# An RWKV pair loop written out flat, its state update folded into one operation, and a bias table made at the start of a hybrid layer

## The reference, cut to what matters

```python
def _wkv_step(S, inp):                                  # RWKV-7: 16 heads, state 64 x 64
    r, w, k, v, a, b = inp
    sa = jnp.einsum('bhvk,bhk->bhv', S, a)
    S = S * w[:, :, None, :] + sa[..., None] * b[:, :, None, :] + v[..., None] * k[:, :, None, :]
    return S, jnp.einsum('bhvk,bhk->bhv', S, r)

def one_block(args):                                    # sparse attention, a block of 128 queries
    ...
    score = jnp.einsum('bths,bth->bts', jax.nn.relu(dots), iws)
    _, idx = lax.top_k(score, topk)
    ...
    logits = jnp.einsum('btngd,btsnd->btngs', qg, ks) * (HD_B ** -0.5)
    bias = rel_bias[_t5_bucket(idx - ps[None, :, None])]
    logits = jnp.where(sel_ok, logits + bias, -jnp.inf)

mixed = (gates[:, :, 0] * (o_a @ lw['p_a']) + gates[:, :, 1] * (o_b @ lw['p_b'])
         + gates[:, :, 2] * (o_m @ lw['p_m']))
h = x + mixed @ lw['w_o']
h = h + _hier_moe(_rmsnorm(h, lw['g_ffn']), lw)
```

## Time and profile before

| | us |
|---|---|
| median of 3 runs | 2541.69 |
| lowest and highest run | 2533.03, 2544.68 |
| profiled execution, its time | 2558.45 |
| its span (first to last instruction) | 2556.9 |
| PE busy | 2334.8 (91%), 13394 matmul instructions |
| DVE, ACT, POOL busy | 532.3, 312.4, 43.2 |

### The profile page before, as it was taken

One profiled execution on the slowest core, in us unless ns is written; L12 is line 12 of the kernel. 1 busy time (PEld: TensorE's weight loads), 2 busy tenths in 40 slices (PEclk: granted clock), 3 DMA queues, 4 the chain that ended last, 5 costly groups with the idle time before them and its releaser, 6 DMA issues.

```text
span 2556.9 us, 32554 instructions
## 1 busy us (share of the span) xinstructions
PE 2334.8 (91%) x13394; PEld 1612.1 (63%) x13394; DVE 532.3 (21%) x1457; ACT 312.4 (12%) x696; POOL 43.2 (2%) x88
## 2 busy tenths in 40 slices
PE   6999999947998999999999999999798999899887
PEld 4887776725756776776777777777454554455444
DVE  1000001233553232232232232200400111011103
ACT  4010001112222011011010110000201100010002
POOL 0000000001000000000000000000000000000000
PEclk9999999968887999999999999999879978897998
DMA  7554443343221323133133232344159769576972
GB/s 236 179 165 132 133 122 121 99 70 113 79 66 39 100 72 104 46 124 104 35 103 102 70 101 99 130 132 173 49 205 364 280 254 373 227 308 273 365 307 88
DMA packets 222911, 392.57 MB, mean 154 GB/s; under 512 B 10784, under 2 KB 165200, under 8 KB 221664
## 3 DMA queue, kind: packets, MB, share of 16 engines
q1 hardware_dynamic: 217712, 382.16, 42.1%
q0 software_dynamic: 3984, 7.83, 1.6%
q10 hardware_dynamic: 1088, 0.66, 0.1%
HBM read 382.32 MB, written 8.29 MB: 153 GB/s over the span
## 4 chain that ended last, share of the span: by engine, by line
PE 82%; DMA 6%; DVE 3%; ACT 2%; issue 2%; another core or an unknown queue 2%; DVEq 1%; ACTq 0%; POOL 0%; SPq 0%
PE bank L822 15%; PE bank L662 10%; PE bank L1035 7%; PE bank L684 7%; DMA ring<-in_w 5%; PE bank L824 5%; PE bank L1054 5%; PE bank L965 5%; PE bank L1083 5%; PE bank L635 4%; PE bank L953 3%; PE bank L1104 2%; PE bank L878 1%; PE bank L886 1%
## 5 line engine op out<-in xcount | busy, mean ns | idle before, releaser
L822 PE MATMUL bank<-uT,ring 128*128 128x288 f32 x1536 | 420.2, 424 | 0.0
L822 PEld LDWEIGHTS bank<-uT,ring 128*128 128x128 f32 x1536 | 290.2, 195 | 84.7 <-issue 4.4
L662 PE MATMUL bank<-uT,ring 128*128 128x288 f32 (+2 forms) x1024 | 248.9, 406 | 0.7 <-ACTq L315 0.7
L662 PEld LDWEIGHTS bank<-uT,ring 128*128 128x128 f32 (+2 forms) x1024 | 190.5, 186 | 58.8 <-ACTq L315 0.9
L684 PE MATMUL bank<-uT,ring 128*128 128x288 f32 x768 | 215.5, 428 | 0.0
L1035 PE MATMUL bank<-SC,Z 128*128 128x128 f32 (+1 forms) x768 | 184.9, 385 | 8.9 <-ACT SC L1389 5.6
L1054 PE MATMUL bank<-ring,Z 128*64 128x512 f32 x768 | 172.1, 604 | 17.0 <-DMA ring<-in_w 15.7
L684 PEld LDWEIGHTS bank<-uT,ring 128*128 128x128 f32 x768 | 148.0, 200 | 44.4 <-issue 6.6
L1035 PEld LDWEIGHTS bank<-SC,Z 128*128 128x128 f32 (+1 forms) x768 | 141.7, 247 | 51.2 <-issue 34.9
L1054 PEld LDWEIGHTS bank<-ring,Z 128*64 128x64 f32 x768 | 64.1, 139 | 122.9 <-issue 122.6
L824 PE MATMUL bank<-Z,ring 128*128 128x288 f32 x512 | 138.9, 417 | 2.0 <-issue 2.0
(11 more groups left out here) (339 smaller groups left out, 2208.1 us busy)
## 6 DMA issues: line engine op xcount, KB each, us to landing
ring<-in_w SPq DMA_DIRECT2D x64, 2048.0 KB, 18.1
ring<-in_w_in SPq DMA_DIRECT2D x102, 1024.0 KB, 7.8
SC<-in_w SPq DMA_DIRECT2D x32, 2048.0 KB, 15.9
ring<-in_w_mem_kv SPq DMA_DIRECT2D x16, 1024.0 KB, 10.1
ring<-in_w_o SPq DMA_DIRECT2D x16, 1024.0 KB, 7.7
ring<-in_p_b SPq DMA_DIRECT2D x8, 1024.0 KB, 5.6
ring<-in_p_m SPq DMA_DIRECT2D x8, 1024.0 KB, 8.1
ring<-in_p_a SPq DMA_DIRECT2D x8, 1024.0 KB, 7.4
```

The lines of the kernel that those rows point to most:

```text
L662: ins = mm(bank[t][0:w, 0:T], rslot[q][:, c, w0:w0 + w], uT[:, c, :], start=c == 0, stop=c == KC - 1)
L822: ins = mm(b[:, 0:T], rslot[q][:, c, P * t:P * t + P], uT[:, c, :], start=c == 0, stop=c == last - 1)
```

## The change

**The pair loop.** All five engines' loops over the pairs are Python loops now, so the instructions of eight pairs stand one after the other, and wait targets are constants. The loops of the other stages stay.

**The state update.** A vector `sx` is made once in a pair (`ee[c] * em[c+1]` for the chunks 0 to 2, `ee[c]` for 3 and 4). After `rw_s0` DVE makes `S1 = S0 * sx[c]`. When the increment has come, one operation makes `bank4 * sx[c] + S1`.

**The order of heads.** Where two or three matmuls of one head stood together (L906 and L907, L919 and L920, L923 to L925), first both heads' first matmul is issued, then both heads' second.

**Two dense groups.** Five groups instead of four stand before `rw_hat`, and one stands after the last chunk's outputs, ahead of `rw_fin`. Three are left after the variance.

**The bias.** `onehot`, `relb` and `brow` lie in `NK` now, which stage 5 alone uses otherwise. They are loaded first of all, the two matmuls are PE's first work (banks 0 and 1), the copies DVE's first, and POOL writes `bias_rows` once `xT_done` is set, at the end of the first transposes. Only the eight loads of `E` wait for stage 3's end.

```diff
-        brow = cut(SC, 0, BW)
-        onehot = cut(SC, BW, BW)
-        relb = cut(SC, 2 * BW, 8)
         NK_t = sb("NK", PAIRS * T)
         vis = cut(NK_t, 0, 2 * TP)
+        brow = cut(NK_t, 2 * TP, BW)
+        onehot = cut(NK_t, 2 * TP + BW, BW)
+        relb = cut(NK_t, 2 * TP + 2 * BW, 8)
...
+            pload(onehot[0:32, :], a["onehot"], "past_in")
+            pload(relb[0:32, :], a["rel_bias"], "past_in")
             for k in (1, 2, 3, 4):
                 phase_end(pool, k)
+            pool.wait_ge(s("brow_done"), 1)
             pload(vis, a["visible"], "past_in")
-            phase_wait(pool, 3)
...
+            pool.wait_ge(s("xT_done"), 1)
             pload(dram_bias, brow[0:H_B, :].unsqueeze(1).to_broadcast([H_B, P, BW]), "brow_out")
             pool.wait_ge(s("brow_out"), 16)
-
+            phase_wait(pool, 3)
             for h in range(H_B):
...
+            pe.wait_ge(s("past_in"), 32)
+            mm(bank[0][0:H_B, 0:512], relb[0:32, :], onehot[0:32, 0:512], start=True, stop=True)
+            mm(bank[1][0:H_B, 0:BW - 512], relb[0:32, :], onehot[0:32, 512:BW], start=True, stop=True).then_inc(s("prep_mm"), 1)
...
-            pe.wait_ge(s("past_in"), 48)
             pe.wait_ge(s("past_hw"), 64)
...
-            mm(bank[7][0:H_B, 0:512], relb[0:32, :], onehot[0:32, 0:512], start=True, stop=True)
-            mm(bank[3][0:H_B, 0:BW - 512], relb[0:32, :], onehot[0:32, 512:BW], start=True, stop=True).then_inc(s("prep_mm"), 1)
-            pe.wait_ge(s("prep_done"), 2)
+            ins.then_inc(s("prep_mm"), 1)
+            pe.wait_ge(s("prep_done"), 1)
...
-            with pe.Fori(0, PAIRS) as j:
+            for j in range(PAIRS):
...
-                merge_mms(4)
+                merge_mms(5)
...
                     for hs in halfs:
                         mm(bank[2][hs, 0:CH], RA[hs, c, 0, :], S0[hs, :], start=True, stop=False)
+                    for hs in halfs:
                         ins = mm(bank[2][hs, 0:CH], Gm[hs, c, 1, 0:CH], tokm[hs, c, :], start=False, stop=True)
...
                 ins.then_inc(s("rw_y"), 1)
+                merge_mms(1)
...
+                V.tensor_tensor(vec["sx"][:, 0:3], vec["ee"][:, 0:3], vec["em"][:, 1:4], ALU.mult)
+                V.tensor_copy(vec["sx"][:, 3:5], vec["ee"][:, 3:5])
...
                     dve.sem_inc(s("rw_s0"), 1)
+                    V.tensor_scalar(S1, S0, vec["sx"][:, c:c + 1], None, ALU.mult)
...
-                    V.tensor_tensor(S1, S0, bank[4][:, 0:CH], ALU.add)
-                    dr()
-                    if c < 3:
-                        V.tensor_scalar(S0s[:, (c + 1) % 2, :], S1, vec["ee"][:, c:c + 1], vec["em"][:, c + 1:c + 2], ALU.mult, ALU.mult)
-                    else:
-                        V.tensor_scalar(SF[:, c - 3, :], S1, vec["ee"][:, c:c + 1], None, ALU.mult)
+                    after = S0s[:, (c + 1) % 2, :] if c < 3 else SF[:, c - 3, :]
+                    V.scalar_tensor_tensor(after, bank[4][:, 0:CH], vec["sx"][:, c:c + 1], S1, ALU.mult, ALU.add)
```

More of the change, by code:

```diff
@@ L151, in build @@
                         ("omka", 8), ("ss", 5), ("rs", 5), ("iw", 48),
-                        ("mx8", 8), ("nmax", 4), ("sum", 4), ("rsum", 4), ("last", 54), ("em", 5), ("ee", 5),
+                        ("mx8", 8), ("nmax", 4), ("sum", 4), ("rsum", 4), ("last", 54), ("em", 5), ("ee", 5), ("sx", 5),
                         ("eps", 2)):
@@ L428, in _ @@
                 strip(R_PAIR + q, merge_strips(0, q))
-            with sp.Fori(1, PAIRS) as j:
+            for j in range(1, PAIRS):
                 for q in range(4):
                     sp.wait_ge(s("mg_mm"), 10 * j + (MG_LAST[q] - 10))
-                    settle(sp)
                     for d_, s_ in merge_strips(j, q)(q):
@@ L521, in _, with pload @@
             pool.memset(vec["eps"][:, 0:1], LNX_EPS)
+            def pload(dst, src, name):
+                return pool.dma_start(dst, src).then_inc(s(name), 16)
+            pload(onehot[0:32, :], a["onehot"], "past_in")
+            pload(relb[0:32, :], a["rel_bias"], "past_in")
             for k in (1, 2, 3, 4):
                 phase_end(pool, k)
-            def pload(dst, src, name):
-                return pool.dma_start(dst, src).then_inc(s(name), 16)
+            pool.wait_ge(s("brow_done"), 1)
             pload(vis, a["visible"], "past_in")
-            phase_wait(pool, 3)
-            pload(onehot[0:32, :], a["onehot"], "past_in")
-            pload(relb[0:32, :], a["rel_bias"], "past_in")
-            pool.wait_ge(s("brow_done"), 1)
+            pool.wait_ge(s("xT_done"), 1)
             pload(dram_bias, brow[0:H_B, :].unsqueeze(1).to_broadcast([H_B, P, BW]), "brow_out")
             pool.wait_ge(s("brow_out"), 16)
+            phase_wait(pool, 3)
             for h in range(H_B):
@@ L565, in pair_in @@
                 cs = bass.ds(j * P, P)
-                if not isinstance(j, int):
+                if j:
                     pool.wait_ge(s("rw_lora"), j)
@@ L583, in _ @@
             pair_in(0)
-            with pool.Fori(0, PAIRS - 1) as j:
+            for j in range(PAIRS - 1):
                 pair_in(j + 1)
@@ L1310, in _ @@
             A(kn, kn, ACT.Sqrt).then_inc(s("kn_rt"), 1)
-            with act.Fori(0, PAIRS) as j:
+            for j in range(PAIRS):
                 def gate(u):
@@ L1431, in _ @@
             V.memset(vec["ss"], 1.0).then_inc(s("ss_init"), 1)
+            dve.wait_ge(s("prep_mm"), 1)
+            V.tensor_copy(brow[0:H_B, 0:512], bank[0][0:H_B, :])
+            V.tensor_copy(brow[0:H_B, 512:BW], bank[1][0:H_B, 0:BW - 512])
+            dr()
+            dve.sem_inc(s("brow_done"), 1)
             for k, part in enumerate((slice(0, 3), slice(3, 5))):
@@ L1599, in bc @@
                 return ap.unsqueeze(1).to_broadcast([P, n, ap.shape[-1]])
-            with dve.Fori(0, PAIRS) as j:
+            for j in range(PAIRS):
                 def pv(name):
```

10 lines of the change are left out of this document (2 added, 8 removed).

## The result

The changed kernel takes 2455.66 us in the median of 4 runs (2453.21 to 2471.07), the kernel before 2543.18 beside it (4 runs, 2533.03 to 2564.01): a ratio of 0.9658, 95% interval 0.9586 to 0.9731, some 87 us faster. The forecast was 2468, with 2448 to 2490 as its range. The time lies inside and the sign is right, but the sum behind it holds errors that cancel, and by the traces some 10 of the 87 us lie behind the last stage that the change touches.

What follows compares the result with a forecast made beforehand. PE is full nearly everywhere, so only its idle or low-clock time can be won: 39.7 + 2.3 - 1.6 + 18.3 + 9.9 + 4.3 + 1.0 = 73.9 us off the 2541.7 median gives 2468 us, range 2448 to 2490.

Steps and rivals of the forecast that it cites:

- wait for E, bias matmuls: Around stage 4: writing `bias_rows` 400 us earlier removes DVE's 39.7 us wait and 2.3 us of bias matmuls.
- state update: Pair loop: one operation behind the increment saves 0.31 us in 32 chunks, 9.9 us; bounds 6.4 and 12.1.
- groups, with the one ahead of `rw_hat`: Pair loop: group ahead of `rw_fin` covers 5.4 us, net 4.3 after mode changes; group ahead of `rw_hat` covers 1.0.
- The other rivals: Stalls stay, 2486 us (0.15); new wait at pair's head, 2476 (0.10); bias late, 2508 (0.03); slower, up to 2580 (0.03).
- The wait ahead of L906's successor 0.1 us or less.: Pair loop: sign that PE's wait for DVE's new state, 12.1 us over 32 times before, nearly goes.
- That cover holds.: Stage 1: beside the 53.8 us write, at 22.5 us a strip, the ring falls back 1.5 of three strips; no loss.
- a strip that PE waits for in the first 130 us: Stage 1: listed among the signs that would prove the prediction wrong.
- strips starve: Stage 1 rival: write and strips slow each other to twice their times; 32 us lost, 2500 us; chance 0.07.
- 1.6 us lost: Stage 4: E loads beside the index-key loads delay the keys by 4.8 - 3.2 = 1.6 us; bounds 0 and 5.2.
- 18.3 us: Pair loop: gain from removing jumps and the lower clock behind them, 16.95 in six pairs plus 1.3; bounds zero and 18.3.
- the pair taken as clean: Pair loop: the last pair, 99.20 us at clock 1.0, less the longest stall, 1.6, gives 97.6 without a jump.
- So I take zero: Pair loop: alternating heads at L906 and L907 gains between zero and 4.8 us; zero taken, 0.26 seeming mostly mode change.

Runs made afterwards that it cites:

- both repairs: Changed kernel with the bias write made from 128 partitions at its early place and E loads held until the index keys land: 2445.34 us, ratio 0.9679.
- the second profile: The kernel before, unchanged, profiled once more: pair loop 807.8 us, stage 4 to the first pair 283.0, experts 669.0 against 705.8 in its first profile.

## Why the prediction was right, and where it was wrong

| term | forecast, us | measured, us | by |
|---|---|---|---|
| wait for E, bias matmuls | 42.0 | 38.6 to 43.4 | both repairs: 244.4 from stage 4 to the first pair, against 283.0 and 287.8 before |
| keys beside E | -1.6 | -2.9 (-2.3 to -4.9 over all profiles) | L727; the keys put first |
| write beside stage 1 | 0 | -5.9 | L636; the write moved, and made wide |
| jumps | 18.3 | 25.0 (27.1 against the second profile) | loops written out only |
| state update | 9.9 | 10.3 | undone alone |
| groups, with the one ahead of `rw_hat` | 5.3 | 5.5 | undone alone |
| order of heads | 0 | 2.2 | undone alone |

**Right.** What bounds the kernel was read right: the wait at L1556 and the jump were the two large ones, and both went whole. The state update and the groups came within 0.4 us, each with some luck. For the update I had taken the merged operation at L1717's 0.22 us; it took 0.28, and the drain, which I had not counted, went too. In the groups' 5.3 us stands 1.0 for the wait ahead of `rw_hat`, which is gone with the jumps already: PE's waits list none there with the loops written out alone, nor with the groups back. The other rivals fell: no new wait stands at the pair's head, E is not late, and the "issue" that the waits list within the written-out pairs, 0.2 us at L905 once in each, stood at L906 before.

**"The wait ahead of L906's successor 0.1 us or less."** This sign did not come: 32 waits make 6.6 us, 0.2 each. With the old order of heads only 1.6 us are left, so the sign failed because alternation brings PE there sooner, which I had not put into it.

**"That cover holds."** This step failed, and with it the zero of the moved write. It took 22.5 us for a strip beside the write from the earlier trace rows, a median of two loads. One of them took 35.0 us, as the DMA view of 550 to 578 us before shows, so the other took 2 x 22.5 - 35.0 = 10.0:

```profile
ring<-in_w_in SPq DMA_DIRECT2D x1, 1024.0 KB, 35.0
```

SP's timeline has the issues of both:

```profile
547.79 5.23 SPq L420 DMA_DIRECT2D ring<-in_w_in  x2
```

The long one landed at 547.79 + 35.0 = 582.8 or later, when the write (done before 577.86) had ended. So neither load measures a strip beside the write: by the packets of stage 1 half of a strip passes at once, and the rest waits for nearly all that is left of the write. Three strips ahead are 3 x 13.9 = 41.7 us, from 58.8 to 100.5. The write held on until 44.8 + 54.8 = 99.6, and the strip came at 104.2. I had named a strip that PE waits for in the first 130 us as a sign of error, and it came. The rival "strips starve" had the place right and a price of 32 us; it cost 5.9, since the write itself was hardly slowed (54.8 us against 53.8) where the rival doubled it.

**"1.6 us lost" for the keys.** Mis-sized: 2.9 in the first profiles, 2.3 to 4.9 over all. I had set E's own landing against the keys'. By the Trainium skill's turn-taking (DMA: Bandwidth & Descriptors, Queues, rings and completion order) I had named 3.2 as the worst; that comes nearer, and some profiles lie beyond it.

**"18.3 us" for the jumps.** Mis-sized: 25.0. The step that failed is the pair taken as clean: 99.20 us less the longest stall, 97.6. With the jump away a pair takes 96.8, so in that pair 2.4 us go and not 1.6. The lower clock is not what I had missed there: it stayed at 1.00. The view above shows 0.5 us more, the wait for DVE at L857, which the written-out pairs do not have; the other 0.3 are not accounted for. Six pairs make 6 x (97.6 - 96.8) = 4.8 of the 6.7 us missed, and the rest lies outside these six.

**"So I take zero" for the heads.** The bound from zero to 4.8 held the 2.2, but I had looked at W1, where nothing changed, and not at the outputs of the last chunk, behind which PE no longer waits.

**The total.** The terms up to the experts add to 73.9 in the forecast, and the two pairs of profiles show 77.0 and 73.9. The equality is luck: 6.7 us more from the jumps and 2.2 from the heads stand against 5.9 lost in stage 1 and 1.3 more at the keys. The time came out 12 us lower than forecast. 87.5 us between the medians less 77.0 leave 10.5 behind the last stage that the change touches, which by the profiles are the experts; the runs behind the medians have no traces of their own to show it.

## What to carry to other kernels

A transfer that moves to a quiet place must be costed by the rate that it leaves to its neighbours, not by the landing time of a neighbour that outlived it; the write from 8 partitions kept 7.6 of 16 DMA engines full for 55 us, and from 128 partitions it was six times quicker and harmless. A short loop's jump cost more than the stall that the trace shows, in most pairs a lower clock behind it and in some another wait; take a pair without any jump as the clean one, or say that there is none. When one operation gets shorter, look at what its neighbours wait for then: a sign put on one wait fails as soon as another edit moves it. And compare the stretches that a change touches before the whole times: here a stretch that it does not touch varied by 37 us from one execution of the same kernel to another.

## What the runs showed of the hardware that was not expected

- Two DMA queues moved 139 and 130 packets in 14 us side by side, one for one, but 0.71 and 0.13 MB: the queue with the longer packets took the engines, and a load of 1024 KB beside it took 33.2 us where 6.8 is the median before.
- One 2560 KB write took 54.8 us from 8 partitions and 8.9 from 128; a packet of 5.1 KB occupied an engine for 0.77 us and for 0.21.
- A wait of 3.79 us on PE was followed by a window of 10 us at a granted clock of 0.71, and 2.75 us of slower work; the jump's 1.4 us in the third pair by one of 0.52, and its 1.6 us in the last by one of 1.00, with the same burst of weights.
- In the experts whole windows of 50 us run at 0.69 to 0.77, none, one or three of them in an execution, 12 to 13 us each, in a code that does not change.
